# High weight parts as one 512-column matmul into both halves of a PSUM bank, in a two-block transformer kernel on one core

## The reference, cut to what matters

```python
def _swiglu(h, wg, wu, wd):
    return (jax.nn.silu(h @ wg) * (h @ wu)) @ wd          # 1024 -> 2816 -> 1024, eight times in all

for l in range(DEPTH):                                    # the second stack; the first is alike
    x = x + 0.5 * _swiglu(_rmsnorm(x, ffn_pre_norm[l]), ...)
    x = x + mixer(_rmsnorm(x, mix_norm[l]), ...)
    x = x + 0.5 * _swiglu(_rmsnorm(x, ffn_post_norm[l]), ...)
```

## Time and profile before

| | |
|---|---|
| median of 3 runs | 2406.56 us (2395.4 to 2407.18) |
| profiled execution, its own time | 2406.13 us |
| span of its instructions | 2404.3 us |
| busy: PE / PEld / DVE / ACT | 2291.9 / 2197.9 / 1537.7 / 1184.5 us |
| mean granted TensorE clock | 0.978 of full speed |
| HBM read | 389.34 MB |

### The profile page before, as it was taken

How to read it: one execution, slowest core, us unless ns; L and a number is a source line. 1 busy time by engine, 2 the same in 40 slices (tenths; PEclk the granted TensorE clock), 3 DMA queues, 4 the chain that set the end, 5 groups by cost and what they waited for, 6 DMA issues and landing times.

```text
span 2404.3 us, 44793 instructions
## 1 busy us (share of the span) xinstructions
PE 2291.9 (95%) x18446; PEld 2197.9 (91%) x18446; DVE 1537.7 (64%) x2216; ACT 1184.5 (49%) x1747; POOL 129.8 (5%) x146
## 2 busy tenths in 40 slices
PE   6999998889999999998999999998999999998998
PEld 6999876879999999787999999986999999998998
DVE  5766647566666765776666666667665666666664
ACT  5644434555446544445554544444544544426543
POOL 2000000110001001000100000100100000001001
PEclk9999987899999999999999999999999999999999
DMA  7556422326555557343455655642655565543653
GB/s 236 190 180 185 149 70 93 106 88 198 184 189 184 189 185 228 106 144 120 141 194 183 196 183 180 219 141 72 192 184 182 180 191 180 162 141 106 194 188 110
DMA packets 383369, 393.27 MB, mean 164 GB/s; under 512 B 6512, under 2 KB 381424, under 8 KB 383040
## 3 DMA queue, kind: packets, MB, share of 16 engines
q1 hardware_dynamic: 381248, 383.30, 49.9%
q0 software_dynamic: 1920, 7.11, 1.0%
HBM read 389.34 MB, written 1.05 MB: 162 GB/s over the span
## 4 chain that ended last, share of the span: by engine, by line
PE 87%; DVE 6%; ACT 4%; issue 1%; POOL 1%; DMA 1%; SPq 0%; POOLq 0%; ACTq 0%; DVEq 0%
PE acc L531 25%; PE acc L535 25%; PE acc L532 24%; PE wide L674 2%; PE acc L549 2%; PE acc L551 2%; PE acc L550 2%; ACT w_hi L815 1%; PE wide L647 1%; DVE w_lo L1048 1%; DVE hn_lo L1080 1%; POOL t L1432 1%; PE wide L663 1%; DMA raw<-in_ffn_w_in 1%; PE wide L602 1%
## 5 line engine op out<-in xcount | busy, mean ns | idle before, releaser
L815 ACT ACTIVATE w_hi<-raw 128x1024 fp32r<-128x1024 f32 (+1 forms) x742 | 768.7, 1040 | 963.8 <-PE acc L535 864.2
L1048 DVE TENSOR_TENSOR w_lo<-raw,w_hi 128x1024 fp32r<-128x1024 f32 (+1 forms) x742 | 889.2, 1201 | 536.1 <-ACT w_hi L815 533.2
L531 PE MATMUL acc<-hn_hi,w_hi 128*128 128x256 f32 x3536 | 855.7, 283 | 37.3 <-DMA colc<-in_cols 18.3
L532 PE MATMUL acc<-hn_lo,w_hi 128*128 128x256 f32 x3536 | 846.2, 280 | 0.0
L531 PEld LDWEIGHTS acc<-hn_hi,w_hi 128*128 128x128 f32 x3536 | 671.2, 190 | 50.7 <-DMA colc<-in_cols 18.3
L532 PEld LDWEIGHTS acc<-hn_lo,w_hi 128*128 128x128 f32 x3536 | 671.5, 190 | 0.5
L535 PE MATMUL acc<-hn_hi,w_lo 128*128 128x256 f32 x3536 | 482.1, 279 | 0.0
L535 PEld LDWEIGHTS acc<-hn_hi,w_lo 128*128 128x128 f32 x3536 | 442.2, 189 | 0.0
L531 PE MATMUL acc<-hid_hi,w_hi 128*128 128x256 f32 x1408 | 334.5, 278 | 0.0
L532 PE MATMUL acc<-hid_lo,w_hi 128*128 128x256 f32 x1408 | 334.5, 278 | 0.0
L532 PEld LDWEIGHTS acc<-hid_lo,w_hi 128*128 128x128 f32 x1408 | 265.3, 188 | 0.0
(11 more groups left out here) (199 smaller groups left out, 2036.4 us busy)
## 6 DMA issues: line engine op xcount, KB each, us to landing
raw<-in_ffn_w_in SPq DMA_DIRECT2D x88, 1024.0 KB, 5.1
raw<-in_ffn_w_out SPq DMA_DIRECT2D x32, 1024.0 KB, 5.2
raw<-in_ffn_pre_w_gate SPq DMA_DIRECT2D x22, 1024.0 KB, 5.3
raw<-in_ffn_pre_w_up SPq DMA_DIRECT2D x22, 1024.0 KB, 5.3
raw<-in_ffn_post_w_gate SPq DMA_DIRECT2D x22, 1024.0 KB, 5.3
raw<-in_ffn_post_w_up SPq DMA_DIRECT2D x22, 1024.0 KB, 5.3
raw<-in_x_w_kv SPq DMA_DIRECT2D x16, 1024.0 KB, 5.4
raw<-in_ffn_pre_w_down SPq DMA_DIRECT2D x16, 1024.0 KB, 5.1
```

The source lines that it names most:

```text
L531: nc.tensor.matmul(bank, wh[:, j, :], a_hi[:, u.k0 + j, :], start=u.first and j == 0, stop=False)
L532: nc.tensor.matmul(bank, wh[:, j, :], a_lo[:, u.k0 + j, :], start=False, stop=False)
L815: nc.scalar.activation(w_hi[:, u.slot, 0:u.nk, :], raw[:, u.raw % RING, 0:u.nk, P * u.half:P * u.half + P], ACT.Copy).then_inc(w_hi_ready, 1)
L1048: nc.vector.tensor_tensor(w_lo[:, u.slot, 0:u.nk, :], raw[:, u.raw % RING, 0:u.nk, P * u.half:P * u.half + P], w_hi[:, u.slot, 0:u.nk, :]. ...
```

## The change

Each pair of activation buffers becomes one tensor with the high part first and the low part second, so that the two stand as 2 x 256 columns in one access pattern. A matmul with the high weight then moves all 512 columns and writes a whole bank: high x high into the first half, high x low into the second. The product with the low weight still moves 256 columns and adds to the first half. The two halves are added outside: ACT copies the second half to SBUF (`copy_cross`), DVE adds that to the first half (`add_cross`), and then does what it did with the bank before. In residuals after a mixer DVE adds both halves to `x` one after the other, with no copy. T units stay as they were. Within a fresh unit each low-weight matmul now stands right behind its wide one; in the others the eight still follow.

```diff
-        hn_hi = sb("hn_hi", [P, KB, T], F32R)
-        hn_lo = sb("hn_lo", [P, KB, T], F32R)
...
+        hn = sb("hn", [P, 2, KB, T], F32R)
...
+        cross = sb("cross", [P, BANKS, T])
...
                 if u.mode == "F":
                     wh, wl = w_hi[:, u.slot], w_lo[:, u.slot]
-                    bank = out_ap(u.out)
+                    both, bank = acc[:, u.out % BANKS, :].rearrange("p (s t) -> p s t", s=2), out_ap(u.out)
+
+                    def low(j):
+                        return nc.tensor.matmul(bank, wl[:, j, :], a[:, 0, u.k0 + j, :], start=False,
+                                                stop=u.last and j == u.nk - 1)
+
                     for j in range(u.nk):
                         if fresh:
                             pe.wait_ge(r_hi, 8 * u.need + j + 1)
                             pe.wait_ge(r_lo, 8 * u.need + j + 1)
-                        nc.tensor.matmul(bank, wh[:, j, :], a_hi[:, u.k0 + j, :], start=u.first and j == 0, stop=False)
-                        nc.tensor.matmul(bank, wh[:, j, :], a_lo[:, u.k0 + j, :], start=False, stop=False)
-                    pe.wait_ge(w_lo_ready, i + 1)
-                    for j in range(u.nk):
-                        mm = nc.tensor.matmul(bank, wl[:, j, :], a_hi[:, u.k0 + j, :], start=False,
-                                              stop=u.last and j == u.nk - 1)
+                        nc.tensor.matmul(both, wh[:, j, :], a[:, :, u.k0 + j, :], start=u.first and j == 0,
+                                         stop=False)
+                        if fresh:
+                            if j == 0:
+                                pe.wait_ge(w_lo_ready, i + 1)
+                            mm = low(j)
+                    if not fresh:
+                        pe.wait_ge(w_lo_ready, i + 1)
+                        for j in range(u.nk):
+                            mm = low(j)
...
+            def copy_cross(i):
+
+                act.wait_ge(unit_done, i + 1)
+                o = units[i].out
+                nc.scalar.activation(cross[:, o % BANKS, :], cross_ap(o), ACT.Copy).then_inc(cross_out, 1)
...
+            def add_cross(out, i, rows=slice(0, P)):
+
+                dve.wait_ge(unit_done, i + 1)
+                dve.wait_ge(cross_out, crossed[i])
+                o = units[i].out
+                return nc.vector.tensor_tensor(out, out_ap(o)[rows], cross[rows, o % BANKS, :], ALU.add)
...
                         if u.src == "hid":
-                            link(nc.vector.scalar_tensor_tensor(hidf[:, k % 2, :], out_ap(u.out), scale, rstd[:, 0, :],
+                            link(add_cross(hidf[:, k % 2, :], n))
+                            link(nc.vector.scalar_tensor_tensor(hidf[:, k % 2, :], hidf[:, k % 2, :], scale, rstd[:, 0, :],
                                                                 ALU.mult, ALU.mult))
...
-                            nc.vector.tensor_tensor(x[:, k, :], x[:, k, :], out_ap(u.out), ALU.add).then_inc(out_evac, 1)
+                            link(nc.vector.tensor_tensor(x[:, k, :], x[:, k, :], out_ap(u.out), ALU.add))
+                            nc.vector.tensor_tensor(x[:, k, :], x[:, k, :], cross_ap(u.out), ALU.add).then_inc(out_evac, 1)
...
                 def scaled(h):
-                    dve.wait_ge(unit_done, u0 + h + 1)
-                    nc.vector.tensor_tensor(silu_g[:, h, :], out_ap(units[u0 + h].out), rstd[:, 0, :], ALU.mult)\
-                        .then_inc(gate_evac, 1)
+                    link(add_cross(silu_g[:, h, :], u0 + h))
+                    nc.vector.tensor_tensor(silu_g[:, h, :], silu_g[:, h, :], rstd[:, 0, :], ALU.mult).then_inc(gate_evac, 1)
```

More of the change, by code:

```diff
@@ L2 @@
 from contextlib import ExitStack
+from itertools import accumulate
 import numpy as np
@@ L182, in build @@
         freed.append((kind, count[kind]))
+    name_of = {i: name for name, l in lin.items() for i in range(l.u0, l.u1)}
+    crossed = list(accumulate(u.last and u.mode == "F" and (u.src == "hid" or name_of[i][:3] not in ("mix", "xo0", "xo1"))
+                              for i, u in enumerate(units)))
     last_of_load = {u.raw: i for i, u in enumerate(units)}
@@ L221, in build @@
         pos = sb("pos", [P, T], I32)
-        with nc.sbuf_tensor("hid_hi", [P, HB, T], F32R) as hid_hi, nc.sbuf_tensor("hid_lo", [P, HB, T], F32R) as hid_lo:
-            pass
+        cross = sb("cross", [P, BANKS, T])
+        with nc.sbuf_tensor("hid", [P, 2, HB, T], F32R) as hid:
+            hid_hi, hid_lo = hid[:, 0], hid[:, 1]
         work = sb("work", [P, 2 * HB, T])
@@ L444, in out_ap, with cross_ap @@
             return acc[:, o % BANKS, 0:T]
+        def cross_ap(o):
+            return acc[:, o % BANKS, T:2 * T]
         def wait_free(eng, o):
@@ L450, in wait_free @@
                 eng.wait_ge((gate_evac, hid_mul, out_evac)[kind], n)
-        name_of = {i: name for name, l in lin.items() for i in range(l.u0, l.u1)}
         def dest_ap(i):
@@ L822, in take @@
                         state.evac = freed[units[i].out][1]
+                        if units[i].mode == "F":
+                            copy_cross(i)
                     split_after(i)
@@ L871, in residual @@
                     u = units[n]
+                    if u.last and u.src == "hid":
+                        copy_cross(n)
                     if n < l.u1 - 1:
@@ L1058, in take @@
                     if name == "af":
-                        ins = nc.vector.tensor_tensor(forget_z(0), ps[0:8], rstd[0:8, 0, :], ALU.mult)
+                        link(add_cross(forget_z(0), i, slice(0, 8)))
+                        ins = nc.vector.tensor_tensor(forget_z(0), forget_z(0), rstd[0:8, 0, :], ALU.mult)
                     elif name == "ga":
-                        ins = nc.vector.tensor_tensor(t2[96:128, 6, :], ps[96:128], rstd[96:128, 0, :], ALU.mult)
+                        z = t2[96:128, 6, :]
+                        link(add_cross(z, i, slice(96, 128)))
+                        ins = nc.vector.tensor_tensor(z, z, rstd[96:128, 0, :], ALU.mult)
+                    elif u.mode == "F" and u.src == "mn":
+                        ins = add_cross(dest_ap(i), i)
                     elif u.src == "mn":
@@ L1064, in take @@
                     elif u.mode == "F":
-                        ins = nc.vector.tensor_tensor(dest_ap(i), ps, rstd[:, 0, :], ALU.mult)
+                        link(add_cross(dest_ap(i), i))
+                        ins = nc.vector.tensor_tensor(dest_ap(i), dest_ap(i), rstd[:, 0, :], ALU.mult)
                     else:
@@ L1167, in mul @@
                         dve.wait_ge(hid_lo_ready, m0 - 1 + h)
-                    nc.vector.tensor_tensor(hidf[:, h, :], silu_g[:, h, :], out_ap(units[u0 + 2 + h].out),
-                                            ALU.mult).then_inc(hid_mul, 1)
+                    link(add_cross(hidf[:, h, :], u0 + 2 + h))
+                    dve.wait_ge(silu_done, m0 + h + 1)
+                    nc.vector.tensor_tensor(hidf[:, h, :], silu_g[:, h, :], hidf[:, h, :], ALU.mult).then_inc(hid_mul, 1)
                 def low_hid(h):
```

18 lines of the change are left out of this document (9 added, 9 removed).

## The result

| | before | after |
|---|---|---|
| median | 2404.52 us (2395.4 to 2407.18, 4 runs) | 2429.8 us (2427.69 to 2436.16, 4 runs) |
| ratio, 95% interval | | 1.0116 (1.0082 to 1.0151) |
| span of the profiled execution | 2404.3 us | 2426.4 us |
| matmuls and weight loads | 18446 each | 12990 each |

The account below looks back on a forecast made before the run. PE bounds the kernel, its narrow stream by weight loads and a small handover. From 2406.1 us, 78 saved by wide matmuls and 16 added on the path give 2344, own range 2315 to 2365, eight in ten 2312 to 2392.

Parts of the forecast that it names:

- the 215.6 ns of a wide matmul: High-weight steps: one wide matmul takes 215.6 ns in place of two narrow ones at 230.4, saving 14.8 ns a step.
- the 80.7 us: Gain on PE from wide matmuls: 5456 high-weight steps at 14.8 ns each, of which 78 us were counted.
- The second rival: A wide matmul is no cheaper than two narrow ones, additions stand alone: 2422 us, from 227.5 ns a wide one; chance 0.06.
- Its two reasons: Wide matmuls: columns of this type, or the jump between the two runs, cost more than a cycle each.
- The reading of the earlier trace, that narrow streams are bound by weight loads: PE's narrow streams: weight loads of about 107 to 110 ns and a small handover set the 115.2 ns, not columns.
- its upper bound: Wide matmuls: if the slow stretch's 117.4 ns were everywhere, the gain is 19.2 ns a step, 105 us.
- The first rival: The 8.5 ns beyond columns are a fixed price of each matmul: PE gains 46 us, time 2377; chance 0.13.
- The bound from below: Wide matmuls: 46 us if the 8.5 ns are a fixed price; nothing if a wide one costs two narrow ones.
- +31 for longer chains: Copies and additions lengthen waits at down projections, mixers, woven units and memory norms; part of the +16 us on the path.
- -15 for fresh units: Fresh units do seven low-weight matmuls while waiting, 0.8 us each, at down projections and behind mixers; part of the +16 us.
- What hid the additions in the up phases: Up phases: DVE needs 9.3 us of each chunk's 10.6, 88%, so the additions fit with little left.
- all marks but the first: Signs in the trace: first, wide matmuls 215 to 217 ns apart; then narrow pace, weight loads, DVE and ACT busy, waits, pauses.

Follow-up runs that it names:

- the bench: TensorE alone, streams of matmuls that compute nothing of the reference, varied by width, type, order and place in SBUF; 256 fp32r columns took 120.0 ns at no shift.
- experiment 1: Changed kernel with high and low parts side by side for each block, so a wide matmul moves one run of 512 columns: 2429.95 us, ratio 1.0079.
- experiment 4: TensorE alone by width, type and place, also with other engines busy, no kernel computed: fp32r 120.0, 173.3 and 226.7 ns for 256, 384 and 512 columns.
- experiment 6: Changed kernel without copies and additions, keeping wide matmuls and the new fresh order; high-weight by low-activation product left out: 2406.28 us, ratio 0.9966.
- experiment 3: Kernel before with only the new order in fresh units, each low-weight matmul behind its block's two high-weight ones: 2397.9 us, ratio 0.9943.
- experiment 2: Changed kernel with each wide matmul split into two narrow ones; copies, additions and order stay: 2432.12 us, ratio 1.0101.
- experiment 7: Changed kernel with copies and waits for them but no additions; high-weight by low-activation product left out: 2410.29 us, ratio 0.9987.
- experiment 14: Kernel before with the new order in fresh units and all tensors 192 bytes further, distance of 64 kept: 2403.55 us, ratio 0.9961.

## Why the prediction was wrong

**The step that failed is the 215.6 ns of a wide matmul.** I took it from plain fp32, "since they have the same weight load and a stream of the same length". The type counts: an fp32r matmul pays 13.3 ns beyond its columns in the bench, a plain fp32 or bf16 one 2.4. In the kernel wide ones average 233 ns, and the 80.7 us were not there. The second rival had a wide one as dear as two narrow ones, decided from 227.5 ns on, and the time it gave (2422) came within 8 us. Its condition held. The closeness of the time is partly luck, since the costs that it adds were not what was measured (below). Its two reasons did not: columns run at one a cycle, and the jump is free (experiments 1 and 4). The sentence of the Trainium skill on non-contiguous patterns (Advanced Engine Details and Errata, PSUM Cachelines) points to the right outcome, but for a moving operand in two runs no run here shows such a slowing: 226.7 ns in one run and in two.

**The reading of the earlier trace rows, that narrow streams are bound by weight loads, is not shown right.** Where the load is taken to set the pace (128 columns in the bench) it is 111.6 ns, but narrow matmuls are 120 ns apart at one placement and 116.7 at another, with the same loads. Only the faster pace of the kernel, 113 ns, is close enough to leave the reading open. And the 115.2 ns of the prediction was a mean of two paces, 113.1 and 117.4, of which it used the slower for its upper bound alone. The first rival, a fixed price of each matmul, is what the bench shows (13.3 ns at every width). In the kernel it fails too: narrow ones pay 6.7 or 11 there (113 or 118 ns, by phase), wide ones 20. The bound from below that I had set, nothing, is what was measured: experiment 6 against 3 is a loss of 5 us, not told from zero.

**The new evacuation was right in kind; its size depends on what is compared.** Forecast: +31 for longer chains and -15 for fresh units, +16. By the ratios copies cost 5 us, additions 31 (22 with the ratio of experiment 1) and the new order -14; experiment 2 puts the whole at 1.0101, +24 us, with an interval from 6 to 43 that holds the 16. PE's pauses in F units say less: 48.8 us before, 38.0 with the new order, 38.1 with the wide matmul, 44.1 with the copies, 56.3 with the additions. That is -10.8, 0, +6.0 and +12.2, together +7.5. The forecast had the terms in about this proportion, and as pauses each of them too large. The pauses that I can name are these: down projections grew by 0.34 us in seven places and 1.1 in the last, against 0.6 and 1.4; the two memory norms by 0.9 each, where I had 1.5; rotations and scan by 1.0 to 1.3, where I had 0.93. They make 9 us, and shorter pauses behind the mixers give some back.

**A term that the prediction did not have is the granted clock.** In the runs of experiment 1 the time follows it: 2422.37 us at 0.974 and 2431.77 at 0.968. At that rate the 0.003 between the means of the kernel before (0.973) and of the change (0.970) are worth some 5 us of the 25, an estimate. Whether the longer pauses lower the clock is not shown.

**What hid the additions in the up phases held.** DVE is busy 72% (76 forecast), ACT 56% (60), PE has no wait in the steady stretches, and weight loads fell as forecast. The profile after came near all marks but the first, 215 to 217 ns, and that one carried the sum.

Sum by what was measured, in ratios: the new order 0.9943, the wide matmul +0.0023, copies +0.0021, additions +0.0129, together 1.0116. It closes by construction, since each is a difference of neighbours. Each difference has an error of some 0.004, so the wide matmul and the copies are not told from zero by it.

**A version that beats both kernels** is the kernel before with the new order in its fresh units alone: 0.9943, and 0.9961 in experiment 14, each clear of 1.

**Still open.** In the kernel before, phases run at 113 or at 118 ns with the same addresses, and its own runs spread from 2395 to 2433 us over all measurements, while the wide ones of experiments 6 and 7 spread by 7 and 12 us. What picks the pace at the start of a phase was not found, nor why wide ones come as 226, 236, 231 and 236 in the kernel. Nor is it known why fp32r pays more than bf16, or why the distance between weights and activations matters; the kernel was tried at distances 0, 64 and 96 only.

## What to carry to other kernels

Before fewer, wider instructions are bought with work on another engine, measure the wide one in the same data type, at the kernel's own addresses and in its own order: a row of another type with the same weight load was 17 ns off, and the whole gain was 15. Price an added addition at each place where a phase waits for the last output; that cost came here although the engine was idle a quarter of the time. The free part of a change (here the order in fresh units) deserves a run of its own. Compare the granted clocks of two profiles before their difference is put down to the change: here two thirds of the 22 us between the spans lay outside the pauses and the pace of the changed part.

## What the runs showed of the hardware that was not expected

- fp32r matmuls pay by the instruction: 120.0, 173.3 and 226.7 ns for 256, 384 and 512 columns, 13.3 over the columns at 2.4 GHz (distance 0); bf16 pays 2.4 (109.1 and 215.8).
- The distance of weights and activations in SBUF, modulo 256 bytes, changes this: 116.7 to 123.3 ns for a narrow one. In the kernel it moved the whole time by 33 us (2420.95 to 2453.68).
- After a change of width five fp32r matmuls are slower before the pace settles, at distance 0 (233, 236, 228, 233, 231, then 226 to 227), and none with the weights moved by 16 bytes; strict alternation is worst (236, 113, 233, 117, 241, 120). bf16 shows none of it.
- fp32r matmuls of 128 columns with a new weight load each start 111.6 ns apart, 58 ns more than their columns.
- A moving operand in two runs 8 KB apart costs as much as one run, 226.7 ns.
